# Two of four expert groups on gathered rows: selection products in the last stage of a two-model kernel

## What is computed

```python
g_sel = jnp.argmax(g_logits, axis=-1)                  # one group of four
top_p, top_i = lax.top_k(e_prob, TOP_K_IN_GROUP)       # two experts of its four
combine = jnp.sum(jax.nn.one_hot(expert_id, N_EXPERTS) * weights[..., None], axis=1)
for e in range(N_EXPERTS):
    h = jax.nn.silu(xt @ w_gate[e]) * (xt @ w_up[e])
    y = y + combine[:, e:e + 1] * (h @ w_down[e])
```

## Time and profile before

| | us |
|---|---|
| median of 3 runs | 2101.05 (2099.2 to 2101.59) |
| the profiled execution | 2099.84 |
| its span | 2098.1 |
| TensorE busy | 2013.7 (96%) |
| VectorE busy | 1476.3 (70%) |
| ScalarE busy | 1015.6 (48%) |
| the expert stage | from about 1810 to the end |

### The profile page before, as it was taken

How to read it: one execution, slowest core, us unless ns; L and a number is a source line. 1 busy time by engine, 2 the same in 40 slices (tenths; PEclk the granted TensorE clock), 3 DMA queues, 4 the chain that set the end, 5 groups by cost and what they waited for, 6 DMA issues and landing times.

```text
span 2098.1 us, 31696 instructions
## 1 busy us (share of the span) xinstructions
PE 2013.7 (96%) x12098; PEld 1741.1 (83%) x12098; DVE 1476.3 (70%) x2255; ACT 1015.6 (48%) x1712; POOL 19.7 (1%) x41
## 2 busy tenths in 40 slices
PE   6999999999999999999998788999999999999998
PEld 4688888888787798888886668999999999888887
DVE  3569667587667579577686787888876688755554
ACT  5362323236667663323234675555554566544444
POOL 0100000000000000000000000000000000000000
PEclk9999999999999999999999899999999999999999
DMA  7857354442111146365673114777455554455553
GB/s 284 321 200 235 128 174 156 159 145 86 61 61 61 41 139 213 127 203 198 224 254 87 40 36 161 243 252 239 127 192 181 164 160 141 141 186 192 183 183 108
DMA packets 254661, 340.38 MB, mean 162 GB/s; under 512 B 24407, under 2 KB 233138, under 8 KB 251458
## 3 DMA queue, kind: packets, MB, share of 16 engines
q1 hardware_dynamic: 254530, 338.60, 48.7%
HBM read 337.52 MB, written 1.05 MB: 161 GB/s over the span
## 4 chain that ended last, share of the span: by engine, by line
PE 80%; DVE 8%; ACT 6%; issue 3%; DMA 0%; DVEq 0%; SPq 0%; ACTq 0%
PE bank L1688 24%; PE bank L1690 24%; PE bank L1689 24%; PE bank L2497 4%; ACT p_raw L1300 1%; DVE w_lo L2568 1%; ACT p_raw L1288 1%; ACT w_hi L953 1%; DVE p_all L3074 1%; DVE norm L2594 1%; PE bank L1740 1%; PE bank L1759 1%; ACT norm L1045 1%; ACT mp_raw L1466 1%; DVE neg_max L3083 1%
## 5 line engine op out<-in xcount | busy, mean ns | idle before, releaser
L2568 DVE TENSOR_TENSOR w_lo<-w_raw,w_hi 128x1024 fp32r<-128x1024 f32 x443 | 540.6, 1222 | 118.4 <-ACT w_hi L1641 84.4
L953 ACT ACTIVATE w_hi<-w_raw 128x1024 fp32r<-128x1024 f32 x350 | 368.0, 1053 | 388.0 <-PE bank L1690 379.6
L1688 PE MATMUL bank<-h_hi,w_hi 128*128 128x512 f32 (+3 forms) x1360 | 466.9, 343 | 14.3 <-DVE h_lo L2604 10.1
L1689 PE MATMUL bank<-h_lo,w_hi 128*128 128x512 f32 (+3 forms) x1360 | 459.6, 338 | 0.0
L1690 PE MATMUL bank<-h_hi,w_lo 128*128 128x512 f32 (+3 forms) x1360 | 459.5, 338 | 0.0
L1688 PE MATMUL bank<-g_hi,w_hi 128*128 128x256 f32 (+1 forms) x1216 | 403.4, 332 | 6.7 <-DVE g_lo L3128 3.5
L1689 PE MATMUL bank<-g_lo,w_hi 128*128 128x256 f32 (+1 forms) x1216 | 399.5, 328 | 0.0
L1690 PE MATMUL bank<-g_hi,w_lo 128*128 128x256 f32 (+1 forms) x1216 | 399.3, 328 | 0.0
L1688 PEld LDWEIGHTS bank<-h_hi,w_hi 128*128 128x128 f32 x1360 | 257.3, 189 | 54.3 <-issue 17.8
L1690 PEld LDWEIGHTS bank<-h_hi,w_lo 128*128 128x128 f32 x1360 | 257.2, 189 | 27.6
L1689 PEld LDWEIGHTS bank<-h_lo,w_hi 128*128 128x128 f32 x1360 | 257.5, 189 | 26.8 <-issue 0.6
(11 more groups left out here) (470 smaller groups left out, 2871.1 us busy)
## 6 DMA issues: line engine op xcount, KB each, us to landing
w_raw<-in_mlp_w SPq DMA_DIRECT2D x128, 1024.0 KB, 5.6
mod_raw<-in_mod_w SPq DMA_DIRECT2D x96, 768.0 KB, 4.8
first_raw<-in_mod_w SPq DMA_DIRECT2D x24, 1024.0 KB, 5.1
w_raw<-in_w_expert_gate SPq DMA_DIRECT2D x32, 512.0 KB, 4.0
w_raw<-in_w_expert_up SPq DMA_DIRECT2D x32, 512.0 KB, 4.9
w_raw<-in_w_expert_down SPq DMA_DIRECT2D x16, 1024.0 KB, 5.0
w_raw<-in_diff_w_qkv SPq DMA_DIRECT2D x12, 1024.0 KB, 5.1
w_raw<-in_fourier_w SPq DMA_DIRECT2D x8, 1024.0 KB, 7.5
```

The source lines that it names most:

```text
L953: act.activation(split_panel(W_hi[n % RING], n), raw_panel(n), ACT.Copy).then_inc(s("w_hi"), 1)
L1688: pe.matmul(dst, w_hi, r_hi, start=start, stop=False)
L1689: pe.matmul(dst, w_hi, r_lo, start=False, stop=False)
L2568: dve.tensor_tensor(split_panel(W_lo[n % RING], n), raw_panel(n), split_panel(W_hi[n % RING], n).bitcast(F32), ALU.subtract).then_inc(s("p ...
```

## The change

Groups 1 to 3 are ranked on chip by their number of tokens. Group 0 (experts 0 to 3 of the order) and the largest of the other three (12 to 15) are computed for all tokens as before. The middle and the smallest (4 to 7 and 8 to 11, "windowed") can't have over 128 tokens each. For them a 0/1 matrix `select` of tokens by slots is made, the normed rows are gathered by products with it (`gather`, from the residual rows split into `xr_hi` and `xr_lo`), and the experts' products are made on one tile of 128 slots. Their down products add up in two banks of their own (`slot_out`); after each group these are split (`slot_rows`) and scattered into `out_ps` by products with the transposed selection (`scatter`). SyncE reads the group numbers into registers and loads the weights of experts 4 to 15 by them. The hidden rows' banks change with expert 12 (`in_bank`, `turn_bank`). The counts, places and the row of slot numbers come from six small products (`group_counts`), with a triangle that GpSimd makes.

The loops of ScalarE carry the same calls as those of VectorE shown at the end, its own part of each.

```diff
+FIRST_WINDOW, LAST_DENSE = 4, 12
...
+def windowed(x):
+    return FIRST_WINDOW <= x < LAST_DENSE
+def tiles_before(x):
+    return sum(1 if windowed(y) else 2 for y in range(x))
...
+            expert_at = list(range(FIRST_WINDOW))
             for x in range(EXPERTS):
+                if x == FIRST_WINDOW:
+                    sp.wait_ge(s("routed"), 4)
+                    most, middle, least = (sp.value_load(group_id[0:1, r:r + 1], min_val=0, max_val=3) for r in range(3))
+                    expert_at += [4 * g + j for g in (middle, least, most) for j in range(4)]
                 first = u + 3 * x - 1 if x else u
                 for half in range(2):
                     k = slice(4 * half, 4 * half + 4)
-                    load_unit(first + half, [(lambda raw: in_rows(raw, 0), w_gate[x][:, k]),
-                                             (lambda raw: in_rows(raw, 1), w_up[x][:, k])])
+                    load_unit(first + half, [(lambda raw: in_rows(raw, 0), w_gate[expert_at[x]][:, k]),
+                                             (lambda raw: in_rows(raw, 1), w_up[expert_at[x]][:, k])])
                 if x:
-                    load_unit(first + 2, [(down_rows, w_down[x - 1])])
-            load_unit(u + 3 * EXPERTS - 1, [(down_rows, w_down[EXPERTS - 1])])
+                    load_unit(first + 2, [(down_rows, w_down[expert_at[x - 1]])])
+            load_unit(u + 3 * EXPERTS - 1, [(down_rows, w_down[expert_at[EXPERTS - 1]])])
...
+            pool.wait_ge(s("x_done"), X_AT["moe"])
+            pool.memset(triangle[:, :], 1.0).then_inc(s("sc_masked"), 1)
+            pool.wait_ge(s("sc_masked"), 3)
+            pool.affine_select(out=triangle[:, :], in_=triangle[:, :], compare_op=ALU.is_ge, fill=0.0, base=0,
+                               pattern=[[1, P]], channel_multiplier=-1).then_inc(s("sc_masked"), 1)
...
             def gates_of(x):
                 act.wait_ge(s("expert_done"), expert_panel(x) + 4)
-                act.wait_ge(s("tok_inv"), 1)
+                act.wait_ge(s("e_rows"), tiles_before(x))
+                if windowed(x):
+                    r = x // 4 - 1
+                    act.wait_ge(s("slots_lo"), 9)
+                    act.activation(e_silu[:, 0, :], in_bank(x, 0)[:, 0:2 * P], ACT.Silu,
+                                   scale=slot_five[:, r, 4:5]).then_inc(s("e_silu"), 1)
+                    return
+                act.wait_ge(s("routed"), 1)
                 for tt in range(2):
-                    if x:
-                        act.wait_ge(s("e_rows"), 2 * x + tt - 1)
-                    act.activation(e_silu[:, tt, :], in_ps[tt][:, 0:2 * P], ACT.Silu,
+                    act.activation(e_silu[:, tt, :], in_bank(x, tt)[:, 0:2 * P], ACT.Silu,
                                    scale=rstd_tok[:, tt:tt + 1]).then_inc(s("e_silu"), 1)
...
+            def slot_rows(r):
+                act.wait_ge(s("expert_done"), expert_panel(8 + 4 * r) + 6)
+                for half in range(2):
+                    act.activation(yw_hi[:, 512 * half:512 * (half + 1)], slot_out[half][:, :], ACT.Copy).then_inc(s("slots_hi"), 1)
...
                 for q in panels:
                     n = p0 + expert_panel(x) + q
                     pe.wait_ge(s("panel_ready"), n + 1)
-                    for tt in range(2):
-                        tok = slice(tt * P, (tt + 1) * P)
+                    for tt in range(1 if windowed(x) else 2):
+                        if x == LAST_DENSE and q == 0 and tt == 1:
+                            pe.wait_ge(s("e_lo"), x)
+                        r = x // 4 - 1
+                        cols = slice(r * P, (r + 1) * P) if windowed(x) else slice(tt * P, (tt + 1) * P)
+                        u_hi, u_lo = (slots_hi, slots_lo) if windowed(x) else (G_hi, G_lo)
                         for k in (2 * q, 2 * q + 1):
                             if x == 0 and tt == 0:
                                 pe.wait_ge(s("h_lo"), SPLIT_AT["ffn_2"] + k + 1)
                             w = slice(k % 2 * 512, (k % 2 + 1) * 512)
-                            ins = split_product(in_ps[tt][:, :], G_hi[:, k, tok], G_lo[:, k, tok], W_hi[n % RING][:, w],
+                            ins = split_product(in_bank(x, tt)[:, :], u_hi[:, k, cols], u_lo[:, k, cols], W_hi[n % RING][:, w],
                                                 W_lo[n % RING][:, w], k == 0, k == KT - 1)
                     ins.then_inc(s("expert_done"), 1)
             def turn_hidden(x):
-                pe.wait_ge(s("e_rows"), 2 * x + 2)
+                pe.wait_ge(s("e_rows"), tiles_before(x + 1))
+                if x == LAST_DENSE:
+                    pe.wait_ge(s("slots_lo"), 13)
+                tiles = 1 if windowed(x) else 2
                 for h in range(2):
-                    for tt in range(2):
-                        ins = pe.transpose(turn_ps[:, h * LAT + tt * P:h * LAT + (tt + 1) * P],
-                                           e_rows[:, tt, h * P:(h + 1) * P], ident[:, :])
+                    for tt in range(tiles):
+                        at_tile = (h * tiles + tt) * P
+                        ins = pe.transpose(turn_bank(x)[:, at_tile:at_tile + P], e_rows[:, tt, h * P:(h + 1) * P], ident[:, :])
                 ins.then_inc(s("e_turned"), 1)
...
+            def slot_product(x, k):
+                n = down_panel(x, k)
+                hi, lo = W_hi[n % RING], W_lo[n % RING]
+                for half in range(2):
+                    w = slice(half * 512, (half + 1) * 512)
+                    for q, (e, v) in enumerate(((E_hi, hi), (E_lo, hi), (E_hi, lo))):
+                        ins = pe.matmul(slot_out[half][:, :], e[x % 2][:, k, 0:P], v[:, w], start=x % 4 == 0 and k == 0 and q == 0,
+                                        stop=x % 4 == 3 and k == 1 and q == 2, skip_group_check=True)
+                return ins
             def expert_out(x):
                 pe.wait_ge(s("e_lo"), x + 1)
+                if x == 0:
+                    pe.wait_ge(s("slots_lo"), 4)
+                if x == FIRST_WINDOW:
+                    pe.wait_ge(s("slots_lo"), 9)
                 for k in range(2):
-                    pe.wait_ge(s("panel_ready"), p0 + expert_panel(x + 1) + 4 + k + 1)
-                    for tt in range(2):
-                        ins = out_product(x, k, tt)
+                    pe.wait_ge(s("panel_ready"), down_panel(x, k) + 1)
+                    if windowed(x):
+                        ins = slot_product(x, k)
+                    else:
+                        for tt in range(2):
+                            ins = out_product(x, k, tt)
                     ins.then_inc(s("expert_done"), 1)
                     if x == EXPERTS - 2 and k == 0:
                         turn_hidden(x + 1)
+            def group_counts():
+                pe.wait_ge(s("routed"), 2)
+                pe.wait_ge(s("sc_masked"), 4)
+                one = r4[2]
+                counts, places = route_ps[:, COUNT_AT:COUNT_AT + 4], route_ps[:, PLACE_AT:PLACE_AT + 8]
+                for tt in range(2):
+                    pe.matmul(counts, ones[:, :], one[:, tt, :], start=tt == 0, stop=tt == 1)
+                pe.matmul(places[:, 0:4], triangle[:, :], one[:, 0, :], start=True, stop=True)
+                pe.matmul(places[:, 4:8], ones[:, :], one[:, 0, :], start=True, stop=False)
+                pe.matmul(places[:, 4:8], triangle[:, :], one[:, 1, :], start=False, stop=True)
+                pe.matmul(route_ps[:, SLOT_AT:SLOT_AT + P], ones[:, :], triangle[:, :], start=True, stop=True).then_inc(s("tok_sum"), 1)
+            def turn_selection():
+                pe.wait_ge(s("routed"), 5)
+                for r in range(2):
+                    for tt in range(2):
+                        ins = pe.transpose(slot_ps[:, r * LAT + tt * P:r * LAT + (tt + 1) * P], select[:, tt, r, :].bitcast(F32), ident[:, :])
+                ins.then_inc(s("slots_ps"), 1)
+            def gather(i):
+                if i == 0:
+                    pe.wait_ge(s("slots_hi"), 5)
+                pe.wait_ge(s("slots_lo"), 4 + i)
+                for k in (2 * i, 2 * i + 1):
+                    dst = slot_ps[:, k % 2 * LAT:(k % 2 + 1) * LAT]
+                    for tt in range(2):
+                        for part, rows in enumerate((xr_hi, xr_lo)):
+                            ins = pe.matmul(dst, rows[:, tt, k * P:(k + 1) * P], select[:, tt, :, :].rearrange("p r c -> p (r c)"),
+                                            start=tt + part == 0, stop=tt + part == 2)
+                ins.then_inc(s("slots_ps"), 1)
+            def slot_weights():
+                pe.wait_ge(s("slots_lo"), 8)
+                for r in range(2):
+                    for tt in range(2):
+                        ins = pe.matmul(slot_ps[:, 5 * r:5 * r + 5], select[:, tt, r, :].bitcast(F32), token_five[:, tt, :],
+                                        start=tt == 0, stop=tt == 1)
+                ins.then_inc(s("slots_ps"), 1)
```

(114 more changed lines are left out.)

79 lines of the change are left out of this document (60 added, 19 removed).

## The result

The changed kernel takes 2046.88 us (median of 4 runs, 2043.73 to 2049.94) where the kernel before took 2100.38 on the same chip: a ratio of 0.9745, 95% interval 0.9728 to 0.9762. Forecast were 2047.8 us, in 2041 to 2060. The profiled execution took 2049.94 us, the longest of the four.

The account below looks back on a forecast made before the run. TensorE alone was taken to bound the expert stage. 67.8 removed - 8.7 added - 3.0 gap - 1.9 clock - 1.0 weights = 53.2 us gained, so 2047.8 us, range 2041 to 2060.

Parts of the forecast that it names:

- What bounds the stage: Expert stage: TensorE alone sets the pace, busy 180.00 of 180.00 us at full clock; DMA share 0.56.
- What is removed: Experts 4 to 11: each loses 24 input matmuls, 12 down matmuls and two transposes, 8.47 us; eight experts, 67.8 us.
- What TensorE gets: Added TensorE work: scattering 3.7 us, gathering 3.8, turned selections and slot-weight products 1.2; sum 8.7 us.
- The ranking: VectorE during expert 1: 26 instructions, 5.4 us, hidden by the weight ring's lead; cost 0, up to 3 us.
- panel 10: Weight panel split behind the ranking during expert 1: split by 14.7 us, wanted by TensorE at 16.6.
- VectorE in the stretch: Windowed experts: six splits, one gating and a halved E_lo take VectorE 7.9 us within 8.48.
- The gap at expert 12: Expert 12's transposes wait until slot_rows(1) empties their bank: TensorE idles 3.0 us, bounds 2.0 and 4.0.
- The clock: After expert 12's gap: about 4 us at the lower clock, nine slower matmuls, 1.9 us, bounds 0 and 4.
- a little longer than that one: Expert 12's 3.0 us gap against an earlier one, TensorE idle 2.5 of 4 us, then granted clock 0.50.
- The weights: Windowed stretch: loads need 9.2 us an expert against 8.48; shortfall 5 us, reserve 6.4; charged 1.0, bounds 0 and 5.
- weights behind: Rival, windowed stretch: sustained load rate between 312 and 256 GB/s, time 2052 to 2067 us; chance 0.15.
- falling clock between experts: Rival: waits before windowed experts bring 1.2 GHz; half the stretch about 2076 us, chance 0.05; all through 2104, 0.02.

Follow-up runs that it names:

- the experiment: For the ranking: changed kernel plus 20 chained memsets ahead of it, 2043.14 us; for the weights: changed kernel plus an unused 512 KB load per windowed expert, 2052.85 us.
- the second trace: Trace of the changed kernel measured again, nothing changed, as base for the other runs: 2044.58 us, ratio 0.9740.
- the extra loads: Changed kernel with another 512 KB loaded for each of the eight windowed experts into a place nobody reads: 2052.85 us, ratio 0.9775.
- the kernel with the longer ranking: Changed kernel with 20 more chained small memsets on VectorE ahead of the ranking: 2043.14 us, ratio 0.9739.
- the kernel with the earlier copies: Changed kernel with the second slot sums emptied before the second of two splits in expert 12, not after both: 2043.98 us, ratio 0.9739.
- the kernel without the gap: Changed kernel with expert 12's transposes moved behind the first input panel of expert 13: 2040.92 us, ratio 0.9721.

## Why the prediction was right, step by step

- *What bounds the stage.* TensorE, before and after. Right, though by less room than is comfortable: the DMA engines are full in the windowed stretch.
- *What is removed.* 8.47 us an expert was forecast, 16.95 - 8.51 = 8.44 measured, 67.5 us for eight instead of 67.8.
- *What TensorE gets.* Scatters 2 × 1.87, gathers 4 × 0.94, turned selections 0.44, slot weights 0.79: 8.7 us, the forecast sum (8.9 by the starts of the matmuls around them). Of the last two, charged at 0.6 each, one was cheaper and one dearer. group_counts took about 1.4 us, not 0.9, nearly all of its cover of 1.48. The distance from the first matmul of the stage to the transposes of expert 0 is 22.03 us in both traces, so it did cost nothing.
- *The ranking.* It ran from 1843.97 to 1849.3, 5.3 us for 5.4 forecast, and stayed hidden. But I named panel 10 as what would come late, and left out the smaller cover, that of e_rows(1), which queues right behind panel 10's split. This cover is 1.8 us by the experiment, where I had 1.9 for another wait.
- *VectorE in the stretch.* 37.96 of 42 us, 7.7 an expert for 7.9 forecast.
- *The gap at expert 12.* 2.76 us idle for 3.0 forecast, through the copies as described; with the clock the pair was forecast at 4.9, and taking both away gave 4.2. Left out of the prediction was the wait for E_lo that the change of banks brings to the inputs of expert 12, 0.1 us here; by the starts the two cost 3.1 us.
- *The clock.* 1.9 us was charged as if certain. Of six traces with this gap of some 2.8 us five show the fall, at a cost of 1.6 us in four of them and 1.3 in the kernel with one windowed group, and one doesn't (below). The bounds, 0 and 4, held this; the reason ("a little longer than that one") was too simple.
- *The weights.* The mis-sized term. I took 9.2 us an expert from two rows; at 355 GB/s it is 8.9. Where 1.0 was charged, a weight load of TensorE waited 0.34 us for w_lo in expert 9, which cost 0.2 us, and the second trace has no such wait. The shortfall is 0.35 us an expert, so 2.5 us of reserve were used; 4.6 were left by the experiment, 7.1 in all for 6.4 reckoned from lead times. But such a sum holds for one execution only: the same place cost 0.5 us in two other traces, and nothing in that of the kernel with the loads in fixed order. It is also not the loads' alone. The late split stands on VectorE right behind the copies of the slot sums, which the prediction had paid for with the scatter, though the scatter comes after it:

```profile
1938.76 1.28 DVE L3845 TENSOR_TENSOR yw_lo<-bank,yw_hi 128x512 fp32r<-128x512 f32 x2
1939.96 0.42 DVE L3814 TENSOR_TENSOR E_lo<-bank,E_hi 128x256 fp32r<-128x256 f32 x1
1940.29 4.62 DVE L2767 TENSOR_TENSOR w_lo<-w_raw,w_hi 128x1024 fp32r<-128x1024 f32 x4
...
1941.56 0.19 PEld L1788 LDWEIGHTS bank<-w_hi,slots_hi 128*128 128x128 f32 x1 [0.34 <-DVE w_lo L2767]
```

- By the Trainium skill (DMA: Bandwidth & Descriptors, Specifications) the rate would be about 358 GB/s. The 355 of this trace agrees, the 364 with the extra loads is a little above it, and the result by that rate, no stall, was nearer than mine.
- *The rivals.* No weights behind, no falling clock between experts: the granted clock is 1.00 from 1909 to 1951. The extra loads did bring waits before several experts, each up to 1.4 us, and the clock stayed at 1.00 even so. The rule of the Trainium skill on oscillation (TensorE: Matmul & The Clock Gate, HAM oscillation) did not come into play; its case has longer waits between shorter bursts than the windowed stretch has in any run here.

Read from the starts, the terms of the trace are 67.5 - 5.2 (gathers, selections and slot weights) - 3.7 (scatters) - 3.1 (expert 12) - 1.6 (clock) - 0.2 (w_lo) = 53.7 us; measured were 53.8, forecast 53.2. The mechanism is the one forecast, and no term is off by more than the weights' 0.8 us. That the median came within 1 us of 2047.8 is partly luck: the runs of one kernel spread over 6 us, and the same kernel's later runs have a median of 2044.58.

## What to carry to other kernels

Halving the work of the bounding engine pays in full only as far as the next resource allows, so work out that resource's time per step and the reserve that stands in rings, and take a sustained rate from a stretch in which it is full. A ring's reserve can be measured: load something useless and see how much of it shows. Where work moves to another bank at the end of a stretch, look for the wait that no earlier stage had, and put other work of the same engine in front of it. To shorten it saves only the time cut off: here the clock fell all the same, at the same cost, after 2.10 us of idle time as after 2.76.

## What the hardware showed that I had not expected

The clock's fall at the same place of the same instructions is not fixed. After a gap of 2.76 us the granted clock was 0.59 over the next 4 us in one trace of the changed kernel and 1.00 in the kernel with the longer ranking; after 2.10 us it fell at once. The same goes for the router's narrow products, which no edit touches: eight of the ten traces have a mean clock of 0.79 from 1810 to 1826, two have 1.00. There the clock falls without a gap: TensorE is busy 4.00 of 4.00 us, with 32 matmuls of 40 and 20 columns. In the changed kernel's second trace two of these products and the granted clock over them (columns as in the earlier trace rows) were

```profile
1816.07 0.35 PE L2714 MATMUL bank<-route,g_hi 128*128 128x40 f32 x1
1816.26 0.37 PE L2715 MATMUL bank<-route,g_lo 128*128 128x20 f32 x1
...
1816.00:1820.00 4.00, 4.00 (x20) 3.93 (x21) 0.00 (x0) 0.15 (x1) 0.00 (x0) 0.51 0.76 249
1820.00:1824.00 4.00, 4.00 (x21) 3.83 (x20) 3.27 (x22) 1.61 (x3) 0.00 (x0) 0.63 0.00 0
```

and in that of the kernel with the earlier copies

```profile
1816.00:1820.00 4.00, 4.00 (x34) 3.87 (x34) 1.50 (x9) 1.54 (x2) 0.00 (x0) 1.00 0.62 220
1820.00:1824.00 4.00, 4.00 (x19) 3.29 (x18) 3.37 (x23) 1.61 (x3) 0.00 (x0) 1.00 0.00 0
```

The first place is worth 1.6 us in one execution and nothing in another. At the router it is 2.7 us, from the stage's first matmul to the transposes of expert 0: 22.03 us at the low clock, 19.30 at the full one. I take it, without having shown it, for a good part of the 4 to 6 us by which runs of one kernel differ; the kernel without the gap also has the narrowest spread but one, 1.6 us.
